# Moving the low parts of the output weights and the masks within two recurrences of a decoder step

## Time and profile before

| | |
|---|---|
| profiled execution | 2119.16 us |
| its span, first to last instruction | 2117.4 us |
| median of three runs | 2122.22 us |
| granted TensorE clock, mean | 0.982 |
| PE busy | 2036.4 us (96%) |
| DVE busy | 1312.1 us (62%) |
| ACT busy | 840.1 us (40%) |
| POOL busy | 282.6 us (13%) |

### The profile page before, as it was taken

How to read it: one execution, slowest core, us unless ns; L and a number is a source line. 1 busy time by engine, 2 the same in 40 slices (tenths; PEclk the granted TensorE clock), 3 DMA queues, 4 the chain that set the end, 5 groups by cost and what they waited for, 6 DMA issues and landing times. The chain is left out here.

```text
span 2117.4 us, 32898 instructions
## 1 busy us (share of the span) xinstructions
PE 2036.4 (96%) x12606; PEld 1828.8 (86%) x12606; DVE 1312.1 (62%) x2265; ACT 840.1 (40%) x1535; POOL 282.6 (13%) x430
## 2 busy tenths in 40 slices
PE   7999999999999799999969999999999799999998
PEld 7999999999999678788649999999999677777774
DVE  5466676555564776766656557676555566666664
ACT  5555543333231544444355344332211443343333
POOL 0000000000000621211100000000000552323222
PEclk9999999999999899999979999999999899999999
DMA  4111133352333654565332332444333544545442
GB/s 139 56 65 54 65 95 92 122 162 89 116 101 101 234 161 149 162 170 152 103 114 75 93 91 83 140 133 132 123 93 105 199 152 169 179 160 180 159 153 72
DMA packets 209222, 264.36 MB, mean 125 GB/s; under 512 B 48228, under 2 KB 156004, under 8 KB 207032
## 3 DMA queue, kind: packets, MB, share of 16 engines
q1 hardware_dynamic: 209080, 262.42, 39.2%
HBM read 172.39 MB, written 89.99 MB: 124 GB/s over the span
## 5 line engine op out<-in xcount | busy, mean ns | idle before, releaser
L568 DVE TENSOR_TENSOR pa_stage<-pa_ps,pa_stage 128x536 f32<-128x536 f32 x110 | 77.1, 713 | 122.9 <-PE pa_ps L535 110.0
L568 DVE TENSOR_TENSOR pc_stage<-pc_ps,pc_stage 128x536 f32<-128x536 f32 x110 | 77.1, 713 | 94.4 <-PE pc_ps L535 73.5
L382 PE MATMUL pa_ps<-a_XT_hi,pa_w_hi 128*128 128x358 f32 x576 | 133.2, 340 | 0.3 <-PEq L201 0.3
L382 PE MATMUL pa_ps<-a_XT_hi,pa_w_lo 128*128 128x358 f32 x576 | 125.9, 327 | 0.0
L382 PE MATMUL pa_ps<-a_XT_lo,pa_w_hi 128*128 128x358 f32 x576 | 125.8, 326 | 0.0
L535 PE MATMUL pc_ps<-c_XT_hi,pc_w_hi 128*128 128x268 f32 x384 | 110.2, 287 | 0.0
L535 PE MATMUL pa_ps<-a_XT_hi,pa_w_lo 128*128 128x268 f32 x384 | 110.1, 287 | 0.0
L535 PE MATMUL pc_ps<-c_XT_hi,pc_w_lo 128*128 128x268 f32 x384 | 110.1, 287 | 0.0
L535 PE MATMUL pc_ps<-c_XT_lo,pc_w_hi 128*128 128x268 f32 x384 | 110.1, 287 | 0.0
L535 PE MATMUL pa_ps<-a_XT_lo,pa_w_hi 128*128 128x268 f32 x384 | 110.0, 287 | 0.0
L535 PE MATMUL pa_ps<-a_XT_hi,pa_w_hi 128*128 128x268 f32 x384 | 109.8, 286 | 0.0
(11 more groups left out here) (589 smaller groups left out, 6120.2 us busy)
## 6 DMA issues: line engine op xcount, KB each, us to landing
pa_w_raw<-in_w_a SPq DMA_DIRECT2D x57, 512.0 KB, 4.6
pc_w_raw<-in_w_c SPq DMA_DIRECT2D x49, 512.0 KB, 4.8
scr_c<-pc_stage SPq DMA_DIRECT2D x48, 512.0 KB, 3.2
scr_a<-pa_stage SPq DMA_DIRECT2D x40, 512.0 KB, 3.2
mc_sample_state<-in_s SPq DMA_DIRECT2D x32, 512.0 KB, 4.6
out_s_s<-mc_sample_state SPq DMA_DIRECT2D x32, 512.0 KB, 2.7
ma_sample_state<-in_c SPq DMA_DIRECT2D x32, 257.0 KB, 4.1
out_c_s<-ma_sample_state SPq DMA_DIRECT2D x32, 257.0 KB, 3.1
```

What stands on the lines that cost most here:

```text
L382: ins = pe.matmul(self.ps[:, 3 * s + t, 0:TC], w[:, k, :], x[:, k, t * TC:(t + 1) * TC], start=(k == 0 and j == 0), stop=(k == KT - 1 and ...
L568: dve.tensor_tensor(dst, self.out(p, product), x, ALU.add).then_inc(self.added, 1)
```

## The change

In the first recurrence DVE's pair of low parts of step n is moved from ahead of step n (pair 0: ahead of the loop; pairs 1 to 3: the end of the step before) into step n, behind the group keys and ahead of the gating product. In the second recurrence POOL makes the stacks 2 to 5 ahead of the masks instead of behind them, and DVE's wait for the masks goes from ahead of the loop into step 0, behind the preparation of head 1. Nothing is added or removed.

```diff
--- before.py
+++ after.py
@@ -2162,7 +2162,6 @@
                                       zs_in[g % 2][:], ALU.mult).then_inc(aux_read, 1)
                 part_a1(0)
                 part_a2(0)
-                O.split_w_lo(dve, 0)
                 dve.wait_ge(pool_chain, A_POOL_LINKS)
                 for n in range(NSTEP):
                     c, h, rows = where(n)
@@ -2196,13 +2195,13 @@
                             mix_samples(g)
                     if n and n % NSEQ == 0 and n < UNITS:
                         group_keys(n)
+                    if n < H:
+                        O.split_w_lo(dve, n)
                     part_m(n)
                     if h == 0 and c:
                         O.post_dve(dve, ps, c - 1)
                     if n < UNITS:
                         sample_state_lo(n)
-                    if n + 1 < H:
-                        O.split_w_lo(dve, n + 1)
                 O.tail_dve(dve, ps, tail)
 
 
@@ -3108,13 +3107,14 @@
                                       ALU.mult).then_inc(mp_ready, 1)
                 part_a(0)
                 O.split_w_lo(dve, 0)
-                dve.wait_ge(pool_chain, POOL_LINKS)
                 for n in range(NSTEP):
                     c, h, rows = where(n)
                     u = unit_of(n)
                     add_state(n)
                     if n + 1 < NSTEP:
                         part_a(n + 1)
+                    if n == 0:
+                        dve.wait_ge(pool_chain, POOL_LINKS)
                     if early_aux(n) and early_aux(n)[0] == "scores":
                         scores(early_aux(n)[1])
                     if n == 0:
@@ -3194,6 +3194,8 @@
                 sample_head(0)
                 for j in range(2):
                     stack_lo(0, j)
+                for j in range(2, 6):
+                    stack_lo(0, j)
                 link = linker(pool, pool_chain)
                 link(pool.memset(qm[:].bitcast(F32), 0.0))
                 for t in range(3):
@@ -3210,8 +3212,6 @@
                 link(pool.affine_select(out=part, in_=part, compare_op=ALU.is_ge, fill=0.0,
                                         base=0, pattern=[[-SLEN, NSEQ], [0, SLEN]], channel_multiplier=1))
                 assert link.count() == POOL_LINKS
-                for j in range(2, 6):
-                    stack_lo(0, j)
                 first_q()
                 O.split_w_lo_pool(pool, 0)
                 for n in range(NSTEP):
```

## The result

The changed kernel takes 2124.56 us (median of 20 runs, 2121.92 to 2128.53), the kernel before 2122.09 (20 runs, 2119.76 to 2126.53). The ratio is 1.0014 with a 95% interval of 1.0008 to 1.0021, that is 1.7 to 4.5 us. By the medians it is 2.5, by the ratio 3.0. The profiled execution has a span of 2121.8 us and a mean granted clock of 0.978 (before 2117.4 and 0.982).

What follows compares the result with a forecast made beforehand. TensorE was taken as the bound, busy 96% of the span. Losses of 5.3 (first recurrence) and 4.0 (second) sum to 9.3 us, on the 2122.22 median giving 2131.5; own range 2127 to 2134, 8 in 10: 2121 to 2136.

Steps and rivals of the forecast that it cites:

- Steps 1 to 3: First recurrence: DVE's pair meets POOL's quarters and alternates with them; pair 3.6 to 3.9 us, round 12.3.
- The term: First recurrence as a whole: predicted loss of 5.3 us, taken from a range of 1.2 to 5.3.
- the two bounds: First recurrence, step 3's gating product: 1.7 us later without DVE and POOL alternating, 5.8 later with it.
- The rival without turns: Both recurrences: DVE's low parts stay 1.2 us beside POOL's quarters; 1.2 + 0 lost, 2123.4 in all; chance 0.20.
- Step 0: First recurrence: pair 0, formerly hidden, now delays the gating product and PE's key product by 2.05 us.
- Second recurrence: POOL's low parts start late, then alternate with DVE's; first output products up to 4.9 us later, stage loses 4.0.
- the give-back: Second recurrence: PE's 1.18 us wait can vanish and POOL's next quarters miss DVE's pair, returning part of the loss.
- The low clock behind the long pause: Second recurrence: PE's pause of 6 us lowers the granted clock, costing up to 1.6 us.
- The clock rival for the first recurrence: First recurrence: longer PE pauses lower the clock into step 4; some 3 us more, 2134.6; chance 0.12.

Runs made afterwards that it cites:

- kernel 1: Kernel before plus only the first recurrence's part of the change, second recurrence as before; ratio to before 1.0002 (0.9993 to 1.0011).
- kernel 2: Kernel before plus only the second recurrence's part of the change, first recurrence as before; ratio to before 1.0012 (1.0003 to 1.0021).
- kernel 3: Kernel before plus the first recurrence's part, but pair 0 left ahead of the loop; ratio to before 0.9996 (0.9987 to 1.0005).
- 4: Changed kernel with each first-recurrence pair one instruction earlier, ahead of the group keys; ratio to before 1.0023 (1.0014 to 1.0032).
- kernel 7: Kernel before with only POOL's second-recurrence masks spread over its waits between the stacks; ratio to before 0.9986 (0.9976 to 0.9995).
- kernel 8: Kernel before with masks spread over POOL's waits, pairs 1 to 3 behind the group keys, pair 0 kept ahead; ratio to before 0.9984 (0.9975 to 0.9993).
- kernel 6: Changed kernel with the first recurrence's group keys and running sum of the samples on all 128 partitions; ratio to before 1.0038 (1.0025 to 1.0052).
- the first two sets: Changed kernel plus 24 trials per set behind its last output, DVE rows beside POOL quarters, varying the row's first instruction; no kernel time given.

## Why the prediction was wrong

- **The failed step** is in "Steps 1 to 3": "In turn, each of DVE's two waits up to 0.7 for a quarter, and each lets POOL's last quarters slip by 1.2 [...]: about 3.6 to 3.9 for the pair, a round of 12.3." The pair took 2.35 and the rounds were 10.55 and 10.86, because an instruction ahead of the pair works on partitions 0 to 95 (the keys) or 0 to 63 (the sum) and POOL then stays out of the row. The term was 5.3; the profiles show 1.7 and 1.9, the runs of the part alone 0.4 (-1.5 to 2.3). With both instructions on 128 partitions the turns are there: 5.2 at step 4 in the one profile, of which 3.3 are theirs (63.36 against kernel 1's 60.08), and 8.1 us in all. The earlier trace rows do show low parts of the same size, but their row begins with a full-width instruction; the choice between the two bounds was made on the operation and its size, and the instruction ahead was not looked at.
- The rival without turns was right for this stage (step 3's product 1.7 later, measured 1.4, and 1.6 in kernel 1) and wrong for the other. Its total, 2123.4, comes nearest to the result, but by another sum than its own 1.2 + 0.
- Step 0 was right: 2.05 forecast, 1.4 to 2.2 in the profiles; PE's L1824 waits 3.49 (before 1.33). The normed head comes 5.76 after the gating product's end, 5.85 forecast.
- **Second recurrence.** POOL's quarters start at 14.67 from the stage's start; the forecast's 1667.5 is 14.55. The turns came as forecast; the first head's low part ends at 26.43, forecast 27.05; the output products come 4.26 later, forecast up to 4.9. What was mis-sized is the give-back. The forecast's 3.0 to 4.6 hold 1.9 for it, beside the 0 to 1.6 for the clock. In this pair of profiles it is 3.4: 4.26 lost at out 0 and 1.64 by the low clock behind it, and yet step 3's output products come only 2.46 later. Single profiles differ by more than that is worth, but the means say the same: out 0 is 22.0 in three profiles with this stage as before and 25.8 in ten with the changed one, out 3 is 63.3 and 65.6. So 3.8 are lost, 1.4 come back and 2.4 remain; the runs of kernel 2 have 2.5. The low clock of the earlier trace rows was counted as a possible extra cost and not as one that could go. Behind the first output products, up to step 3's, the granted clock falls once more (twelve products of 4.6 in place of 3.0) in all three profiles with this stage as before (before, 1 and 3), in those with the changed stage in three of ten. That PE's wait of 1.18 brings it was not tried by itself; it stays open.
- The low clock behind the long pause came: PE waited 5.97, and its products from 1681.40 ran at a granted 0.63, so partly at 1.2 and partly at 2.4 GHz. It had been put at 0 to 1.6. From the start of the first to the end of the last the twelve products took 4.64, which is 1.64 more than the 3.00 of the same twelve in the kernel before; the 2.77 of the earlier trace rows is counted from 0.21 behind the first one's start. The Trainium skill ("TensorE: Matmul & The Clock Gate", What's actually happening) says that the array is at half rate after it was idle, and the trace agrees here.
- The clock rival for the first recurrence: the low stretch at the stage's start is longer in the changed kernel and in 1, 3 and 4 than in before (705 to 718: 0.61 to 0.63 against 0.74), and in 3 it falls on step 0's products. It can't be put to the change, though: kernel 7 has 0.61 with the first recurrence as before, and kernel 8 has 0.74 with that of kernel 3. In step 4, where the rival had it, the clock is at 1.00.

## What to carry to other kernels

Before a price from one place of a trace is used in another, compare the instructions just ahead as well as the instruction itself. Where two bounds lie 4 us apart on one question of contention, the forecast hangs on that question. Fill an engine's gaps with small work instead of moving the work as a block: the block that left the stacks' path came back on the path of the low parts.

## What the runs showed of the hardware that was not expected

DVE and POOL took turns at the port, instruction by instruction, as long as DVE's row was full-width: a subtraction of 1.21 then took 1.74 and a quarter of 0.72 took 1.70 (32 of 32 trial rows of SBUF subtractions on all partitions in the first two sets, without the keys). That the loser waits for the whole instruction is what the Trainium skill says ("SBUF — State Buffer", SBUF: two separate sides), and the trace agrees. Behind an instruction on the first 32, 64, 96 or 112 partitions that POOL meets, POOL waited for DVE's whole row: its quarter took 3.0 to 3.2 beside a pair, and 5.3 to 5.4 beside four subtractions. Why it does so, whether the upper 64 partitions really differ, why a 64-partition instruction three places ahead does it at some starting points and not at others, and what ends the state, stays open.

In the first recurrence it was a gain: kernel 6, without it, is 3.5 later at step 4 than the changed kernel (63.36 against 59.89), and some 5 us slower in the runs, 8.1 against 2.5 to 3.0. POOL has the time there; its long waits cost PE two waits of 0.44 for a head's low part.
